# Mixer entry, sink attention, post-norms and a halved first tile: four edits to a network of two blocks in one kernel

## The reference, cut to what matters

```python
for layer in range(DEPTH):
    g = norm_g[layer]
    h = h + 0.5 * rms_norm(swiglu(rms_norm(h, g[0]), ffn_w_in[layer, 0], ffn_w_out[layer, 0]), g[1])
    u = rms_norm(h, g[2])
    m = rwkv7_time_mix(u, ...) if layer == 0 else swa_sinks(u, k_sh, v_sh, ...)
    h = h + rms_norm(m, g[3])
    h = h + 0.5 * rms_norm(swiglu(rms_norm(h, g[4]), ffn_w_in[layer, 1], ffn_w_out[layer, 1]), g[5])
    if layer == 0:
        kv = rms_norm(h, kv_norm_g) @ w_kv + b_kv
# inside the RWKV mixer, with xx = u shifted by one token minus u:
xr, xw, xk, xv, xa, xg = [u + xx * mu[i] for i in range(6)]
w = f(w0 + tanh(xw @ w1) @ w2); a = sigmoid(a0 + (xa @ a1) @ a2); g = sigmoid(xg @ g1) @ g2
```

## Time and profile before

| | before |
|---|---|
| median of three runs | 2849.88 us |
| the profiled execution | 2848.1 us, span 2846.2 us |
| granted TensorE clock, mean | 0.966 |
| TensorE busy | 2700.0 us, 95% of the span |
| VectorE (DVE), ScalarE (ACT) busy | 1094.9 us (38%), 627.9 us (22%) |
| GpSimd (POOL) busy | 1783.7 us (63%) |
| memory traffic | 225.94 MB, 79 GB/s |

### The profile page before, as it was taken

One profiled execution on the slowest core, in us unless ns is written; L12 is line 12 of the kernel. 1 busy time (PEld: TensorE's weight loads), 2 busy tenths in 40 slices (PEclk: granted clock), 3 DMA queues, 4 the chain that ended last, 5 costly groups with the idle time before them and its releaser, 6 DMA issues.

```text
span 2846.2 us, 47915 instructions
## 1 busy us (share of the span) xinstructions
PE 2700.0 (95%) x17928; PEld 2199.1 (77%) x17928; DVE 1094.9 (38%) x1624; ACT 627.9 (22%) x1203; POOL 1783.7 (63%) x1827
## 2 busy tenths in 40 slices
PE   8999988988987999999999999899999999999998
PEld 7888877767775788888888888678888888777677
DVE  3333043774554533310533303655333224123344
ACT  2111033433532211101211102343111011344211
POOL 6777768673321577776677766665777756645565
PEclk9999989989998999999999999999999989999998
DMA  4333313220000233333233332332333323322212
GB/s 138 95 95 96 96 45 88 75 57 3 4 3 12 74 89 96 95 96 94 75 96 96 96 96 78 115 133 70 97 96 96 95 72 92 90 62 67 76 42 81
DMA packets 116791, 225.94 MB, mean 79 GB/s; under 512 B 13088, under 2 KB 13856, under 8 KB 115616
## 3 DMA queue, kind: packets, MB, share of 16 engines
q1 hardware_dynamic: 114624, 209.46, 26.1%
q10 hardware_dynamic: 2016, 14.22, 1.4%
HBM read 221.53 MB, written 2.10 MB: 79 GB/s over the span
## 4 chain that ended last, share of the span: by engine, by line
PE 70%; DVE 7%; ACT 3%; issue 3%; POOL 3%; DMA 0%; DVEq 0%; POOLq 0%; ACTq 0%; SPq 0%
PE bank L222 17%; PE bank L224 17%; PE bank L223 17%; PE bank L320 1%; PE bank L1290 1%; POOL turn_a L1978 1%; DVE h L692 1%; PE bank L1305 1%; PE bank L353 1%; PE bank L2224 1%; PE bank L1240 1%; PE bank L240 1%; DVE acc L316 1%; PE bank L2215 1%; PE bank L2406 1%
## 5 line engine op out<-in xcount | busy, mean ns | idle before, releaser
L209 POOL TENSOR_TENSOR w_lo<-w_raw,w_hi 128x512 fp32r<-128x512 f32 x778 | 1045.5, 1344 | 755.5 <-PE bank L224 593.1
L222 PE MATMUL bank<-x_hi,w_hi 128*128 128x512 f32 x1904 | 751.5, 395 | 4.3 <-POOL w_lo L209 2.2
L224 PE MATMUL bank<-x_hi,w_lo 128*128 128x512 f32 x1904 | 747.8, 393 | 0.0
L223 PE MATMUL bank<-x_lo,w_hi 128*128 128x512 f32 x1904 | 742.8, 390 | 0.0
L214 POOL TENSOR_SCALAR w_hi<-w_raw 128x512 fp32r<-128x512 f32 x778 | 569.9, 733 | 4.8 <-DMA w_raw<-weights 4.8
L222 PEld LDWEIGHTS bank<-x_hi,w_hi 128*128 128x128 f32 x1904 | 358.2, 188 | 83.6 <-POOL w_lo L209 4.2
L224 PEld LDWEIGHTS bank<-x_hi,w_lo 128*128 128x128 f32 x1904 | 357.9, 188 | 80.2
L223 PEld LDWEIGHTS bank<-x_lo,w_hi 128*128 128x128 f32 x1904 | 358.1, 188 | 79.2 <-issue 0.2
L659 DVE TENSOR_TENSOR f<-bank,rstd 128x512 f32<-128x512 f32 x88 | 56.7, 686 | 595.5 <-PE bank L224 587.7
L222 PE MATMUL bank<-mid_hi,w_hi 128*128 128x512 f32 x704 | 276.4, 393 | 0.8 <-POOL w_lo L209 0.8
L224 PE MATMUL bank<-mid_hi,w_lo 128*128 128x512 f32 x704 | 276.3, 393 | 0.0
(11 more groups left out here) (426 smaller groups left out, 3584.3 us busy)
## 6 DMA issues: line engine op xcount, KB each, us to landing
w_raw<-weights SPq DMA_DIRECT2D x778, 256.0 KB, 2.6
ada_w<-ada_in ACTq DMA_DIRECT2D x8, 1536.0 KB, 6.7
h<-xT SPq DMA_DIRECT2D x4, 512.0 KB, 7.0
out<-f SPq DMA_DIRECT2D x8, 256.0 KB, 2.2
mask_b<-mask_b_in ACTq DMA_DIRECT2D x1, 640.0 KB, 5.2
spread<-spread_in SPq DMA_DIRECT2D x1, 512.0 KB, 7.5
window<-window_in ACTq DMA_DIRECT2D x1, 512.0 KB, 4.0
masks<-masks_in SPq DMA_DIRECT2D x1, 320.0 KB, 7.0
```

The source lines that it names most:

```text
L209: pool.tensor_tensor(w_lo[:, (n - 1) % RW, :], w_raw[:, (n - 1) % RS, :], w_hi[:, (n - 1) % RW, :].bitcast(F32), ALU.subtract).then_inc(w_ ...
L222: pe.matmul(outs[m], w_hi[:, s, c], hi, start=first, stop=False)
L223: pe.matmul(outs[m], w_hi[:, s, c], lo, start=False, stop=False)
L224: done = pe.matmul(outs[m], w_lo[:, s, c], hi, start=False, stop=last)
```

## The change

Four edits are made together.

- **Post-norm at layer ends** (`late=True`): TensorE sums `acc` first and squares 6 and 7 behind it; the last square has its own buffer `sq_last` and waits for no other. The activation table with the square root is loaded at the start of `output_scalar`, and the root comes ahead of the second scaled copy. `update_f` waits for its own tile of f instead of all.
- **Halves**: in front of f1, `swa` and f3 the first tile is scaled, added, made into x_hi and multiplied in two halves of 256 columns.
- **Mixer entry**: the LoRA products take gain*h (split while h is updated), four banks instead of two, and the norm is applied to their outputs on DVE (`lora_in`), where u and u shifted are added. Squares with odd numbers are summed on TensorE, the others on DVE. u tiles are made one by one beside the mixing. POOL folds a unit with one multiplication by a broadcast factor from `segments`.
- **Attention**: the scores of steps 0 to 2 are made between units of the Q projection; the bias goes from DVE to ACT; the low part is made one iteration later; the ada sums are cut in four parts, with two buffers, and ada 4 to 7 lie behind the loop; four units of the output projection are put into the last iterations.

The diff, cut to its core:

```diff
-        def early_products(pe, outs, k, x0, n):
+        def early_products(pe, outs, k, x0, n, halved=0):
...
-            pe.wait_ge(x_hi_ready, x0 + k + 1)
             s = n % RW
-            for m, o in enumerate(outs):
-                c = slice(m * P, (m + 1) * P)
-                pe.matmul(o, w_hi[:, s, c], x_hi[:, k, :], start=k == 0, stop=False)
-                pe.matmul(o, w_lo[:, s, c], x_hi[:, k, :], start=False, stop=False)
+            for t, ready in ((slice(0, T // 2), (x_half, halved)), (slice(T // 2, T), (x_hi_ready, x0 + 1))) if halved and k == 0 else \
+                    ((slice(0, T), (x_hi_ready, x0 + k + 1)),):
+                pe.wait_ge(*ready)
+                for m, o in enumerate(outs):
+                    c = slice(m * P, (m + 1) * P)
+                    pe.matmul(o[:, t], w_hi[:, s, c], x_hi[:, k, t], start=k == 0 and t.start == 0, stop=False)
+                    pe.matmul(o[:, t], w_lo[:, s, c], x_hi[:, k, t], start=False, stop=False)
...
-            j += nm.sq0
-            if j >= 2:
-                square_used(act, j - 2)
-            act.activation(sq[:, j % 2, :], src, ACT.Square, **bias).then_inc(sq_ready, 1)
+            g = nm.sq0 + j
+            if g >= 2 and not (nm.late and j == nm.tiles - 1):
+                square_used(act, g - 2)
+            act.activation(square_at(nm, j), src, ACT.Square, **bias).then_inc(sq_ready, 1)
...
+            sums_of(pe, out, acc, nm.late or not nm.summed, not nm.late).then_inc(sums_ready, 1)
...
             unread(1)
+            norm_sums(pe, s.post, bank[s.post_at][0])
             for k in s.post.summed:
                 sum_square(pe, s.post, k, bank[s.post_at][0])
-            norm_sums(pe, s.post, bank[s.post_at][0])
             unread(2)
             norm_wide(pe, s.post, bank[s.post_at][1])
...
         def output_scalar(act, s):
+            act.preload_act_table_set("sqrt_and_others")
...
-                if m == 3:
+                if m == 1:
                     norm_root(act, s.post, bank[s.post_at][0], D)
...
+            if s.halved:
+                act.wait_ge(h_half, s.halved)
+                act.activation(x_hi[:, 0, 0:T // 2], h[:, 0, 0:T // 2], ACT.Copy, scale=vcol(s.gain_in, 0)).then_inc(x_half, 1)
...
+                if s.halved and k == 0:
+                    act.activation(x_hi[:, k, T // 2:], h[:, k, T // 2:], ACT.Copy, scale=vcol(gain, k)).then_inc(x_hi_ready, 1)
+                    square(act, s.pre, k, h[:, k, :])
+                    continue
...
+            for t, scaled_, added in ((slice(0, T // 2), f_half, h_half), (slice(T // 2, T), tmp_ready, h_ready)):
+                dve.tensor_tensor(f[:, 0, t], f[:, 0, t], bank[s.post_at][1][:, t], ALU.mult).then_inc(scaled_, 1)
+                dve.wait_ge(scaled_, number if t.start == 0 else s.h0 + 1)
+                dve.tensor_tensor(h[:, 0, t], h[:, 0, t], f[:, 0, t], ALU.add).then_inc(added, 1)
...
-                dve.wait_ge(f_ready, s.h0 // 2 + 4)
-                dve.wait_ge(f_late, s.h0 // 2 + 4)
+            if k < 4:
+                dve.wait_ge(f_ready, s.h0 // 2 + k + 1)
+            else:
+                dve.wait_ge(f_late, s.h0 // 2 + k - 3)
             dve.tensor_tensor(f[:, k, :], f[:, k, :], bank[s.post_at][1][:], ALU.mult).then_inc(tmp_ready, 1)
...
-            for k in each:
                 n = s.n_lora + k
                 pe.wait_ge(w_lo_ready, n + 1)
+                pe.wait_ge(*ra("u_hi", k))
+                for m in range(4):
+                    c, t = slice(m * P, (m + 1) * P), slice(1 - m // 2, T + 1 - m // 2)
+                    pe.matmul(sb_[m][:], w_hi[:, n % RW, c], u_hi[:, k, t], start=k == 0, stop=False)
+                    pe.matmul(sb_[m][:], w_lo[:, n % RW, c], u_hi[:, k, t], start=False, stop=False)
+                if k == KT - 1:
+                    sum_square(pe, s.pre, k, sa[0])
+                    norm_sums(pe, s.pre, sa[0])
                 pe.wait_ge(*rv("u_lo", k))
...
+                for m in range(4):
+                    c, t = slice(m * P, (m + 1) * P), slice(1 - m // 2, T + 1 - m // 2)
+                    done = pe.matmul(sb_[m][:], w_hi[:, n % RW, c], u_lo[:, k, t], start=False, stop=k == KT - 1)
                 done.then_inc(w_used, 1)
-            pe.wait_ge(u_ready, KT)
+                if k < KT - 1:
+                    sum_square(pe, s.pre, k, sa[0])
+            norm_wide(pe, s.pre, sa[1])
+            pe.wait_ge(rstd_ready, s.rs + 1)
             for b, set_ in enumerate((SETA, SETB)):
                 if b:
-                    pe.wait_ge(*ra("g_in"))
+                    pe.wait_ge(*rv("back", 1))
...
+            act.wait_ge(*rv("zero"))
+            act.activation(u_hi[:, :, 0:1], u_arr[:, :, 0:1], ACT.Copy).then_inc(*ra.tell("zero_hi"))
             for k in each:
                 act.wait_ge(h_ready, s.h0 - KT + k + 1)
+                act.activation(u_hi[:, k, 1:T + 1], h[:, k, :], ACT.Copy, scale=vcol(s.gain_in, k)).then_inc(*ra.tell("u_hi", k))
...
+            act.wait_ge(u_ready, 1)
+            act.activation(rstd[:], bank[SETA][1][:], ACT.Copy).then_inc(rstd_ready, 1)
             for q in each:
                 tile(q)
-            act.wait_ge(w_used, s.n_k)
-            act.activation(wa_raw[0:64, :], bank[SETB][0][0:64, :], ACT.Tanh).then_inc(*ra.tell("w_in"))
-            act.activation(wa_raw[64:P, :], bank[SETB][0][64:P, :], ACT.Copy).then_inc(*ra.tell("a_in"))
-            act.activation(tg_raw, bank[SETB][1][:], ACT.Sigmoid).then_inc(*ra.tell("g_in"))
+            act.wait_ge(*rv("in", 0))
+            act.activation(wa_raw[0:64, :], wa_raw[0:64, :], ACT.Tanh).then_inc(*ra.tell("w_in"))
+            act.wait_ge(*rv("in", 1))
+            act.activation(tg_raw, tg_raw, ACT.Sigmoid).then_inc(*ra.tell("g_in"))
...
+            update_f(dve, f0, 0)
+            dve.memset(u_arr[:, :, 0:1], 0.0).then_inc(*rv.tell("zero"))
+            dve.wait_ge(*rv("zero"))
+            dve.tensor_copy(u_lo[:, :, 0:1], u_arr[:, :, 0:1]).then_inc(*rv.tell("zero_lo"))
+            for k in each:
+                update_h(dve, f0, k)
+                if k + 1 < KT:
+                    update_f(dve, f0, k + 1)
+                dve.wait_ge(*ra("u_hi", k))
+                dve.scalar_tensor_tensor(out=u_lo[:, k, 1:T + 1], in0=h[:, k, :], scalar=vcol(s.gain_in, k), in1=u_hi[:, k, 1:T + 1].bitcast(F32),
+                                         op0=ALU.mult, op1=ALU.subtract).then_inc(*rv.tell("u_lo", k))
+                add_square(dve, s.pre, k)
             norm_inverse(dve, s.pre)
...
             def u_tile(k):
                 dve.scalar_tensor_tensor(out=u_arr[:, k, 1:T + 1], in0=h[:, k, :], scalar=vcol(s.gain_in, k),
-                                         in1=bank[SETA][1][:], op0=ALU.mult, op1=ALU.mult).then_inc(u_ready, 1)
...
+            def lora_in(step):
+                name, j = (("now", 0), ("back", 0), ("in", 0), ("now", 1), ("back", 1), ("in", 1))[step]
+                o, shifted = (wa_raw, tg_raw)[j], v_arr[:, 2 + j, 0:T]
+                if step == 0:
+                    dve.wait_ge(w_used, s.n_k)
+                if name == "now":
+                    dve.tensor_tensor(o, bank[SETB][j][:], rstd[:], ALU.mult).then_inc(*rv.tell(name, j))
+                elif name == "back":
+                    dve.tensor_tensor(shifted[:, 1:T], bank[SETB][2 + j][:, 1:T], rstd[:, 0:T - 1], ALU.mult).then_inc(*rv.tell(name, j))
+                else:
+                    dve.wait_ge(*rv("back", j))
+                    dve.tensor_tensor(o[:, 1:T], o[:, 1:T], shifted[:, 1:T], ALU.add).then_inc(*rv.tell(name, j))
...
+            u_tile(0)
             dve.wait_ge(*rg("omu", 1))
             mixing(0)
+            dve.wait_ge(rstd_ready, s.rs + 1)
             for q in each:
+                if q + 1 < KT:
+                    u_tile(q + 1)
                 tile(q)
+                if 1 <= q < 7:
+                    lora_in(q - 1)
             dve.wait_ge(*ra("tg_hi"))
             dve.tensor_tensor(wa_lo[:], wa_raw, wa_hi[:].bitcast(F32), ALU.subtract).then_inc(*rv.tell("wa_lo"))
             dve.tensor_tensor(tg_lo[:], tg_raw, tg_hi[:].bitcast(F32), ALU.subtract).then_inc(*rv.tell("tg_lo"))
...
-            for k in each:
-                pool.tensor_scalar(r_gather[:, k, :], gather[:, k, 0:HEADS], vcol("r_k", k), None, ALU.mult).then_inc(*rg.tell("gather", k))
+            for j, i in enumerate(SEGMENTS):
+                source = omu[:, i * KT:(i + 1) * KT] if j < 4 else vec[:, VEC.at[f"mu{i}"]:VEC.at[f"mu{i}"] + KT]
+                pool.tensor_copy(segments[:, :, j:j + 1], source.unsqueeze(2)).then_inc(*rg.tell("segment", j))
...
-                    for j, (i, a, b) in enumerate(((1, 0, 64), (4, 64, 128), (5, 128, 256)) * 2):
-                        factor = omu[:, i * KT + k:i * KT + k + 1] if j < 3 else vcol(f"mu{i}", k)
-                        c = slice(a + 256 * (j // 3), b + 256 * (j // 3))
```

(71 more changed lines are left out.)

117 lines of the change are left out of this document (51 added, 66 removed).

## The result

The changed kernel takes 2812.77 us (median of 4 runs, 2811.36 to 2818.96), the kernel before 2849.45 us (2846.75 to 2850.76): a ratio of 0.9877, 95% interval 0.986 to 0.9894. The forecast was 2813.0 us.

The account below looks back on a forecast made before the run. TensorE, busy 2700.0 of 2846.2 us, bounds the kernel, so gains come only where it stands still, waits or does filler work. -13.5-2.6-0.5-20 = -36.6 takes 2848.1 to 2811.5, on the median 2813 us; range 2797 to 2832.

Parts of the forecast that it names:

- Steps 1 and 2: Mixer entry: one POOL product per fold removes TensorE waits of 8.0 and 0.8 us; DVE has h done at 414.
- Step 3: Mixer entry: u's norm, behind the last hi products, sums, root and wide, is there at 421; first low part at 426.5.
- Step 4: Mixer entry: K's inputs come every 3.8 us with POOL beside; last low part at 453, K's first half ends at 456.
- Step 5: Mixer entry: ACT's tanh, sigmoid, high parts and table loads, 5.0 us, are exposed; K's copies at 457.3, gain 12.5.
- Norm at the ends, -2.6: Layer ends: table load before the squares and root after one scaled copy start the root earlier; -2.6 us, from -1 to -4.
- Halves, -0.5: First tile behind three layer ends: +0.15 us at mixer's end and before attention, -0.8 at attention's end; from +1 to -2.5.
- rival 1: TensorE bounds the attention loop (3.8 a step) and K's inputs keep up (3.0 a tile): 2804 us; chance 0.17.
- Point 5: Attention: four ada sums behind the loop, with DVE's tiles and additions, end level with TensorE: zero taken, up to +3 us.
- 2: DVE and POOL take turns: K's inputs 4.4 a tile, update 3 us longer, attention steps 4.4: 2826 us; chance 0.19.
- 3: Attention loop stays at 4.9 us a step, set by the cycle through POOL, TensorE and copies: 2822 us; chance 0.10.
- 4: Lower TensorE clock in the LoRA stage and K's first half makes the kernel slower than before, 2855 us; chance 0.03.
- 5: Halves and reordered sums give nothing or a loss, worth 3 us; chance 0.03 that all four parts come to nothing.

Follow-up runs that it names:

- e11: Changed kernel with GpSimd's low parts of 48 mixer units made over 64 of 512 columns, the rest left out: 2796.36 us, ratio 0.9824.
- e5: Changed kernel with the old mixer entry; late post-norm, halves and attention stay changed: 2827.53 us, ratio 0.9924.
- e6: Changed kernel with the old attention; late post-norm, halves and mixer stay changed: 2833.51 us, ratio 0.9948.
- e2: Changed kernel with the halves taken out, the first tile behind three layer ends whole again: 2813.02 us, ratio 0.9873.
- e8: Changed kernel with the mixer's normed tile two ahead and GpSimd's gather scalings moved behind K's and V's splits: 2805.84 us, ratio 0.9853.

## Why the prediction was right, step by step

- **Total.** 2813.0 forecast, 2812.8 measured, inside 2806 to 2821. Part of this is luck: the attention gave more, the mixer and the norms less. From the first FFN's last product to K's copies, in the rest of the mixer and in the attention with its end, -12.5, -1 and -20.95 were forecast, together -34.5; they gave -8.1, -0.4 and -24.6 in the first profile and -10.5, -1.8 and -24.4 in the second, together -33.1 and -36.7.
- **Mixer, -13.5.** From the last product of the first FFN to K's copies it is 88.3 us before, 80.2 and 77.8 after: -8.1 and -10.5. The mechanism held. Steps 1 and 2 did: the fold takes 1.04 to 1.47, h is done at 415.0 against 414 forecast, TensorE waits 1.5 once for w_lo in place of 8.0. Step 3, the norm at 421, was 421.87 for the root and 423.8 for the first u; the first low part came at 428.26, 1.8 late. Step 3's own terms, 414+3+3, give 420 and not 421. Step 4 failed in size: 4.10 a tile instead of 3.8, 2.1 us over seven tiles. The wait for the mix was counted; the pace without GpSimd beside was put at 3.6 and is 3.3 with most of its low parts gone, its stretch at 0.2 and is 0.8 (e11). The sum has a slip as well: 2.6 and two terms of 0.6 to 0.7 give 3.8 to 4.0, not 3.6, and the 2.6, read beside GpSimd, held some of its stretch already. Step 5, the exposed tanh and sigmoid before K's copies, took 5.07 as forecast (5.0) and did not end last: the copies wait 0.46 for TensorE's last product and start at 461.20. The 3.9 us by which they are later than 457.3 are the 1.8 and the 2.1. The 1 us that the chain behind was to regain was 0.4 and 1.8.
- **Norm at the ends, -2.6.** The ends of the second, third and last FFN gave 0.7 each (forecast 0.65, 0.65, 0.5); at the second, last product to root is now 1341.33-1337.63 = 3.70 against 1350.16-1345.72 = 4.44. The mixer's end lost 0.3 to 0.5 (forecast 0.1). The first end lost 0.6 to 2.7 up to the update instead of gaining 0.85, and the attention's 0.4 to 0.5 up to the root instead of gaining 0.95: there the running sum was 1.6 and 1.5 late, where the text allowed "here no later" and 0.1 to 0.4. Each term is right by itself: with the old mixer the first end gains 1.1 (e5), with the old attention the attention's end gains 1.1 (e6). What the forecast left out is that the other edits load VectorE there: at the first end the wide fold and the split stretch its two additions to 3.18 us (1.49 in the earlier trace rows and in e5), at the attention's end the ada sums make its tail late.
- **Halves, -0.5.** At the attention's input +0.9 (e2), forecast +0.15: right in sign, and the size six times as large. The -0.8 at the last FFN's input is neither shown nor refuted, for the two pairs of profiles give +1.1 and -1.6. The reason given for the first, VectorE ends last, was right; that an earlier product lets GpSimd split earlier beside VectorE is what the low parts of 1.82 suggest, and was not tried by itself.
- **Attention, -20.** -24.6 and -24.4. First turned product: 1809.14, and with the 7.5 us by which the attention began earlier 1816.7, forecast 1815.9. Steps: 3.73 instead of 4.2; the twelve from 1809.14 to 1852.88 took 43.7 us, forecast 1868.6-1815.9 = 52.7. This is rival 1's bound, TensorE, at a clock of 1.00; in variants with the same loop the clock fell to 0.95 and the loop took up to 2.8 us longer. The last four steps with four units and the twelve units behind took 56.7 us, forecast 53. Point 5, "zero taken, up to +3": 1.5 us, up to 3.8.
- **Rivals.** 1 held in the attention and not in the mixer. 2 held as a mechanism in the mixer (e11) and in VectorE's tail; K's inputs came 0.3 a tile later than forecast, not 0.6. 3 fell: 3.73 a step. 4 fell: the clock is 0.98 from 390 to 412 in the LoRA stage and 0.87 from 422 to K's copies. 5 held in part, as the small one it was: the halves gave nothing at the attention's input, and the reordered sums lost at the first FFN's, the mixer's and the attention's end.
- **Signs.** No wait of VectorE for x_hi in the loop, as said. K's first half ends 8.7 us earlier in the first profile and 12.1 in the second, where 12 to 15 were said; counted with the start of the attention moved by 7.5, the first turned product comes 4.0 us earlier, of 4 to 5.

## What to carry to other kernels

When an engine's waits are removed, look at what stands next in line on the helpers: here VectorE's tail behind the loop became the bound at the attention's end, and its length then varied with a transfer that had been hidden. Sum first what is ready first, judged at each place by itself and with all edits in place: a norm end that gained alone lost once another edit put wide GpSimd instructions beside it. Price VectorE's two-input instructions beside GpSimd's splits at their stretched length. A head start for the first of eight tiles is worth nothing where a helper's pace sets the eighth.

## What the runs showed that had not been expected

- At the first FFN's end the late norm alone gained 1.1 us up to the root (e5). With the wider fold beside it the end became longer than before, up to the update by 0.6 us in one profile and by 2.0 to 2.7 us in seven.
- A 128x512 instruction of VectorE with two SBUF inputs takes 0.68 to 0.75 us alone and mostly 1.09 or 1.77 beside GpSimd's splits; GpSimd's split grows from 1.27 to 1.8 at the same time. With one input in PSUM it stays at 0.68.
- Moving work away from GpSimd (e8) bought nothing, for the next split took its place beside the same VectorE chain.
- Two profiles of one kernel differed by 11.8 us, spread over most of the stretches. An edit of 2 us is read from its own rows, not from the time.
